# Three attentions of a two-block transformer kernel: order of scores, maximum and normalising, and place of a projection

## The chip, the cores and the metric

One core of one Trainium2 chip runs the whole kernel. The metric is the device time of one execution in microseconds, as a median over runs.

## The reference, cut to what matters

512 tokens of width 1024 pass through two transformer blocks in float32. Three attentions lie in them. The first block has a neighbourhood attention (8 heads of 64; every token sees a window of a grid of 8 rows by 64 columns, with a bias per head) and a dilated one (three window and dilation pairs, merged with weights from their log-sums). The second block opens with a differential attention and a pooling mixer side by side:

```python
proj = h @ ab_w_in[e]
q, k, v, u = jnp.split(proj, [DIFF_WIDTH, 2 * DIFF_WIDTH, 3 * DIFF_WIDTH], axis=-1)
a_out = _diff_attention(q, k, v, ab_lambda[e], ab_subln[e], i)
b_out = _pool_mixer(u, pool_w[e], pool_scale[e])
x = x + jnp.concatenate([a_out, b_out], axis=-1) @ ab_w_out[e]
# _diff_attention, for each block of 128 queries, over the keys up to it
p1 = jax.nn.softmax(jnp.where(mask, s1, -jnp.inf), axis=-1)
p2 = jax.nn.softmax(jnp.where(mask, s2, -jnp.inf), axis=-1)
p = p1 - lam * p2
# _pool_mixer, for each of four groups of 128 channels, w = 2, 4, 8, 16
outs.append((cs - lagged) / count[None, :, None] - ug)
```

`lam` comes from two exponentials of dot products of parameters. The attention's output is normalised per head (rms norm), the pooled groups are each multiplied by a 128 by 128 matrix.

## The kernel before, in words

The program is one instruction stream per engine, ordered by hand, with counting semaphores between them. Activations lie transposed, channels on partitions, 512 tokens along. A matrix product takes weight tiles of 512 KB (128 output columns, 1024 rows) through a ring of four places: SP loads a tile (L413) as soon as PE has counted the tile four earlier as done (`tile_done`); ACT rounds it to the high part (`part`, L1089, called by `parts` at fixed places of its stream); GpSimd subtracts to get the low part (`split`, L554, in order of the tiles); PE then multiplies high by high, high by low and low by high, 24 matmuls of 512 columns for a tile (`three`, L613 to L615, in `linear`).

Each attention has 16 steps and the same frame on three engines (`attention`, one function each). On PE, in turn `i`: scores (i), transposes of the probabilities (i-1) (`turn`), output (i-2). On DVE: normalising (i-1) (`norm_p`), then maximum (i) with the bias or mask added on the way out of PSUM (`smax`, L1501, and the negated maximum, L1512), then the copy out (i-2). On ACT: exponential (i) with its sum (L1163, L1319), then the copy (i-1) of the transposed probabilities out of PSUM (L1168, L1324). Scores lie in two buffers of SBUF and two pairs of PSUM banks (0 to 3), the transposes in banks 4 and 5, outputs in 6 and 7.

In the neighbourhood attention (L723 scores, L732 transposes, L743 outputs) every step has 2 x 256 score columns. Its bias tile is refilled by SP once maximum 4 is done and is used from step 12 on; after maximum 16 SP loads the mask of the dilated one into the same place. The dilated attention (L759, L761, L769, L781) has 768 columns a step. In the differential one (L922, L931, L938) a step is one head of one block of 128 queries; steps 0 to 3 have 128 columns in each of the two halves, steps 4 to 7 have 256, 8 to 11 384, 12 to 15 512. Its normalising is a reciprocal (L1760), one scaling for each half (L1763, L1764, the second with lambda) and their sum (L1767).

Ahead of the differential attention PE makes q, k (8 tiles, T_AB to T_AB+7), v (4 tiles) and then `u`, the input of the pooling (tiles T_AB+12 to T_AB+15, `linear`); ACT copies each out (L1308), takes the lambda exponential (L1311) and rounds tiles T_ABO to T_ABO+3 of the output projection. GpSimd splits all these tiles, waits for `u`, and pools the four groups in a row (L594, L595, L599, L601) while the attention runs. Behind it comes, for each of four heads, square (ACT), mean (PE, L950), root (ACT), reciprocal (DVE, L1780), product (L1784), and the pooled group's matmul (L952) and scaling (L1787); each of the eight chunks is split in a high and a low part (L1444), and the output projection (T_ABO, 8 tiles) starts.

## Time and profile before

| what | value |
|---|---|
| median of 3 runs | 3739.52 us (3739.14 to 3746.37) |
| the profiled execution's own time | 3744.43 us |
| its span, first to last instruction | 3742.6 us |
| busy: PE, DVE, ACT, POOL | 93%, 44%, 32%, 34% |
| mean granted TensorE clock | 0.953 of full |
| chain that ended last: PE, DVE, issue, POOL | 68%, 12%, 11%, 4% |

PE is a stream of matmuls, and its busy share is high nearly everywhere; the share of the other engines says only where they work. "Granted clock" is 1.0 at 2.4 GHz and 0.5 at 1.2 GHz; a value between is a mean over time. A group's "idle before" is the time its engine stood still just ahead of it, with the releaser behind the arrow. GpSimd is called POOL in the rows.

### The profile page before, as it was taken

To read this page: it belongs to the slowest core of one execution; us is meant where nothing else is said; L and a number is where in the kernel's file an instruction comes from. 1 tells how busy PE (TensorE), PEld (TensorE's weight loads), DVE (VectorE), ACT (ScalarE), POOL (GpSimd) and SP (SyncE) were. 2 spreads that over 40 slices of the span, in tenths; PEclk is the share of its full clock that TensorE was granted. 3 is DMA by queue.
4 is the path that set the end of the run, shared out by engine and by line. 5 is a ranking of instruction groups with operands and counts; after the bars stand their busy time and mean duration, and the time that the engine had idled before them with its cause. 6 is when DMAs were issued, how large, how long until landed. Compare 5 with 4: busy or idle time off the path is not lost.

```text
span 3742.6 us, 41725 instructions
## 1 busy us (share of the span) xinstructions
PE 3475.5 (93%) x15884; PEld 2786.2 (74%) x15884; DVE 1633.4 (44%) x2894; ACT 1182.6 (32%) x1640; POOL 1276.2 (34%) x550
## 2 busy tenths in 40 slices
PE   7968999999999999999999998858999997969998
PEld 5665777887888888888888875736888686748886
DVE  5805215996545511455555534073322216153221
ACT  4424223333333333222222223332322333033221
POOL 3320133443333334444444432412444332014442
PEclk9988999999999999999999999978999998589999
DMA  2230132343554565766666631302333221012332
GB/s 104 67 101 23 63 100 71 115 144 107 197 180 173 199 202 167 196 185 188 190 184 187 190 118 57 107 1 68 96 96 96 82 80 34 0 45 90 96 96 79
DMA packets 424646, 428.03 MB, mean 114 GB/s; under 512 B 146720, under 2 KB 343968, under 8 KB 422704
## 3 DMA queue, kind: packets, MB, share of 16 engines
q1 hardware_dynamic: 424496, 425.93, 36.4%
q8 instruction: 106, 1.74, 0.2%
q14 instruction: 44, 0.36, 0.0%
HBM read 354.57 MB, written 69.21 MB: 113 GB/s over the span
## 4 chain that ended last, share of the span: by engine, by line
PE 68%; DVE 12%; issue 11%; POOL 4%; ACT 2%; DMA 1%; SPq 1%; POOLq 0%; DVEq 0%; PEldq 0%; ACTq 0%
PE pb L613 19%; PE pb L615 19%; PE pb L614 19%; POOL s_over L554 4%; PE pb L872 3%; PE pb L630 1%; DVE s_hS L1444 1%; DVE s_sq L1430 1%; PE pb L1048 1%; DMA s_ring<-w 1%; PE pb L796 1%; PE pb L1050 1%; PE pb L1038 1%; DVE s_arena L1651 1%; PE pb L781 1%
## 5 line engine op out<-in xcount | busy, mean ns | idle before, releaser
L554 POOL TENSOR_TENSOR s_over<-s_ring,s_rhigh 128x1024 fp32r<-128x1024 f32 x518 | 1253.4, 2421 | 2430.5 <-ACT s_rhigh L1089 2430.4
L1089 ACT ACTIVATE s_rhigh<-s_ring 128x1024 fp32r<-128x1024 f32 x518 | 548.8, 1060 | 1635.9 <-DMA s_ring<-w 803.8
L613 PE MATMUL pb<-s_hS,s_rhigh 128*128 128x512 f32 x2368 | 953.9, 403 | 81.8 <-DVE s_hS L1444 76.9
L615 PE MATMUL pb<-s_hS,s_over 128*128 128x512 f32 x2376 | 932.1, 392 | 0.0
L614 PE MATMUL pb<-s_hS,s_rhigh 128*128 128x512 f32 x2368 | 929.2, 392 | 0.0
L613 PE MATMUL pb<-s_over,s_rhigh 128*128 128x512 f32 x1600 | 632.4, 395 | 0.0
L615 PE MATMUL pb<-s_over,s_over 128*128 128x512 f32 x1600 | 632.0, 395 | 0.0
L614 PE MATMUL pb<-s_over,s_rhigh 128*128 128x512 f32 x1600 | 631.9, 395 | 0.0
L613 PEld LDWEIGHTS pb<-s_hS,s_rhigh 128*128 128x128 f32 x2368 | 449.5, 190 | 201.3 <-DVE s_hS L1444 65.5
L614 PEld LDWEIGHTS pb<-s_hS,s_rhigh 128*128 128x128 f32 x2368 | 450.4, 190 | 95.3 <-issue 7.0
L615 PEld LDWEIGHTS pb<-s_hS,s_over 128*128 128x128 f32 x2376 | 449.6, 189 | 96.2
L1579 DVE TENSOR_TENSOR s_xT<-pb,s_xT 128x512 f32<-128x512 f32 x216 | 149.5, 692 | 700.9 <-PE pb L615 700.9
L614 PEld LDWEIGHTS pb<-s_over,s_rhigh 128*128 128x128 f32 x1600 | 300.4, 188 | 73.1 <-issue 0.2
L613 PEld LDWEIGHTS pb<-s_over,s_rhigh 128*128 128x128 f32 x1600 | 300.4, 188 | 73.0 <-issue 0.2
L615 PEld LDWEIGHTS pb<-s_over,s_over 128*128 128x128 f32 x1600 | 300.3, 188 | 72.9
L1702 DVE TENSOR_TENSOR s_std<-s_arena 128x512 f32<-128x512 f32 x128 | 254.5, 1988 | 85.0 <-DMA s_arena<-gates 83.4
L1805 DVE TENSOR_TENSOR s_std<-s_arena 128x512 f32<-128x512 f32 x64 | 101.2, 1582 | 232.4 <-ACT s_arena L1277 232.4
L1684 DVE TENSOR_TENSOR s_arena<-s_arena 128x1024 f32<-128x1024 f32 x64 | 87.9, 1373 | 231.5 <-PE pb L872 228.0
L1693 DVE TENSOR_TENSOR s_over<-s_std,s_over 128x512 fp32r<-128x512 f32 x192 | 142.8, 744 | 95.7 <-ACT s_over L1220 94.9
L1687 DVE TENSOR_SCALAR s_arena<-s_arena 128x128 f32<-128x128 f32 x512 | 153.5, 374 | 0.0
L872 PEld LDWEIGHTS pb<-s_arena 128*128 128x128 f32 x1024 | 124.1, 191 | 5.0
L1220 ACT ACTIVATE s_over<-s_std 128x512 fp32r<-128x512 f32 x192 | 118.9, 619 | 26.6 <-DVE s_std L1702 12.4
(234 smaller groups left out, 2863.2 us busy)
## 6 DMA issues: line engine op xcount, KB each, us to landing
s_ring<-w SPq DMA_DIRECT2D x272, 512.0 KB, 3.5
s_ring<-eu SPq DMA_DIRECT2D x128, 512.0 KB, 4.0
s_ring<-ev SPq DMA_DIRECT2D x128, 512.0 KB, 4.1
acts<-s_arena SPq DMA_DIRECT2D x128, 256.0 KB, 4.0
gates<-s_arena SPq DMA_DIRECT2D x8, 4096.0 KB, 13.8
s_arena<-acts SPq DMA_DIRECT2D x128, 256.0 KB, 4.4
s_arena<-gates SPq DMA_DIRECT2D x128, 256.0 KB, 4.5
s_xT<-xT SPq DMA_DIRECT2D x1, 2048.0 KB, 8.2
```

Source lines behind the costliest of these rows:

```text
L554: gp.tensor_tensor(rlow[:, s, :, :], ring[:, s, :, :], rhigh[:, s, :, :].bitcast(F32), ALU.subtract).then_inc(S("w_split"), 1)
L613: mm(dst, a_high, b_high, start=start, stop=False)
L614: mm(dst, a_high, b_low, start=False, stop=False)
L615: return mm(dst, a_low, b_high, start=False, stop=stop)
L872: mm(pb[:, 4 + (t // 4) % 4, (t % 4) * P:(t % 4 + 1) * P], oh2[:, t // 8 % 2, t % 8, :], oh1[:, t % 8, :], start=True, stop=True).then_inc ...
L1089: sc.activation(rhigh[:, s, :, :], ring[:, s, :, :], ACT.Copy).then_inc(S("w_high"), 1)
L1220: sc.activation(actS[:, half, 0, k, :], std[:, k % 2, :], ACT.Copy).then_inc(S("e_high"), 1)
L1579: return ve.tensor_tensor(xT[:, c, :], pb[:, bank, :], xT[:, c, :], ALU.add)\
L1687: ve.tensor_scalar(oh1[:, t % 8, :], iota, chT[:, 0, t:t + 1], chT[:, 2, t:t + 1], ALU.is_equal, ALU.mult).then_inc(S("oh_done"), 1)
L1693: ve.tensor_tensor(actS[:, half, 1, k, :], std[:, k % 2, :], actS[:, half, 0, k, :].bitcast(F32), ALU.subtract).then_inc(S("e_act"), 1)
L1702: ve.tensor_tensor(std[:, e % 2, :], va_in[:, e % 4, :], gtile[:, e % 4, :], ALU.mult)\
L1805: ve.tensor_tensor(std[:, j % 2, :], ga[:, j % 2, :], ga[:, j % 2, :], ALU.mult)\
```

## The change

- PE: scores (0) are issued ahead of the loop; turn `i` issues scores (i+1), transposes (i-1), then a piece of other work where there is one (`beside`), then output (i-2).
- DVE: maximum (i) comes first in a turn, then normalising (i-1), then copy out (i-3). Maximum (i) waits for the transposes that free its buffer: three buffers in the neighbourhood and the differential attention, two in the dilated one.
- The four tiles of `u` are projected in quarters (6 matmuls each) inside the turns of the differential attention, into bank 7; its outputs all use bank 6 and each waits for the copy out before. ACT copies group j out in turn 4 (j+1), and rounds T_ABO to T_ABO+2 in turns 6, 10 and 14 and T_ABO+3 behind the last. GpSimd pools a group when it is there and splits one T_ABO tile after each.
- Differential normalising: the sum of both scaled halves becomes one scaling, a product of two 128 x 1 values and one fused product-and-add.
- Scratch of the part behind the attention moves from `ptmp` to `dsc`, and DVE's wait for all four pooled groups ahead of it goes.

```diff
@@ GpSimd
-            splits(T_AB, T_ABO + RING)
+            splits(T_AB, T_ABO)
             gp.wait_ge(S("pool_in"), 32)
-            gp.wait_ge(S("d_copied"), 20)
             for gi in range(4):
+                gp.wait_ge(S("d_copied"), 16 + gi + 1)
...
                 gp.wait_ge(S("pooled"), gi + 1)
+                splits(T_ABO + gi, T_ABO + gi + 1)
@@ PE
-            def attention(n, s0, scores, turn, outp):
+            def attention(n, s0, scores, turn, outp, beside=None):
+                scores(0).then_inc(S("at_scores"), 1)
                 for i in range(n + 2):
-                    if i < n:
-                        if i >= 2:
-                            pe.wait_ge(S("at_max"), s0 + i - 1)
-                        scores(i).then_inc(S("at_scores"), 1)
+                    if i + 1 < n:
+                        if i >= 1:
+                            pe.wait_ge(S("at_max"), s0 + i)
+                        scores(i + 1).then_inc(S("at_scores"), 1)
                     if 1 <= i <= n:
                         pe.wait_ge(S("at_prob"), s0 + i)
                         turn(i - 1).then_inc(S("at_turned"), 1)
+                    if beside is not None and i < n:
+                        beside(i)
...
-            for i in range(4):
-                pe.wait_ge(S("d_copied"), 4 + i + 1)
-                linear(T_AB + 12 + i, i)
-            pe.wait_ge(S("d_copied"), 20)
+            pe.wait_ge(S("d_copied"), 16)
+            def pool_in(i):
+                j, r = divmod(i, 4)
+                n = T_AB + 12 + j
+                if r == 0:
+                    slot(n)
+                    if j >= 1:
+                        pe.wait_ge(S("d_copied"), 16 + j)
+                for c in range(2 * r, 2 * r + 2):
+                    m = three(pb[:, 7, :], rhigh[:, n % RING, c, :], rlow[:, n % RING, c, :], hS[:, 0, c, :],
+                              hS[:, 1, c, :], c == 0, c == DC - 1)
+                if r == 3:
+                    m.then_inc(S("tile_done"), 1)
...
             def diff_out(s):
+                if s >= 1:
+                    pe.wait_ge(S("at_out"), DIFF0 + s)
                 for b in range(i + 1):
-                    m = mm(pb[:, 6 + s % 2, 0:P], ...
+                    m = mm(pb[:, 6, 0:P], ...
@@ ACT
-            for i in range(4):
-                parts(T_AB + 12 + i + 3)
-                sc.wait_ge(S("tile_done"), T_AB + 12 + i + 1)
-                sc.activation(du[:, i, :], pb[:, i, :], ACT.Copy).then_inc(S("d_copied"), 1)
+            parts(T_AB + 15)
             sc.wait_ge(S("lam_dot"), 1)
             sc.activation(lam[:, 2:4], lam[:, 0:2], ACT.Exp).then_inc(S("lam_exp"), 1)
-            parts(T_ABO + 3)
+            def pool_in(i):
+                if i >= 6 and i % 4 == 2:
+                    parts(T_ABO + i // 4 - 1)
+                if i >= 4 and i % 4 == 0:
+                    j = i // 4 - 1
+                    sc.wait_ge(S("tile_done"), T_AB + 12 + j + 1)
+                    sc.activation(du[:, j, :], pb[:, 7, :], ACT.Copy).then_inc(S("d_copied"), 1)
...
+            parts(T_ABO + 3)
             sc.wait_ge(S("at_out"), DIFF0 + 16)
@@ DVE
-            def attention(n, s0, smax, norm_p, outp):
-                for i in range(n + 2):
+            def attention(n, s0, buffers, smax, norm_p, outp):
+                for i in range(n + 3):
+                    if i < n:
+                        ve.wait_ge(S("at_scores"), s0 + i + 1)
+                        if i >= buffers:
+                            ve.wait_ge(S("at_turned"), s0 + i - buffers + 1)
+                        smax(i)
                     if 1 <= i <= n:
                         ve.wait_ge(S("at_exp"), s0 + i)
                         norm_p(i - 1).then_inc(S("at_prob"), 1)
-                    if i < n:
-                        ve.wait_ge(S("at_scores"), s0 + i + 1)
-                        if i >= 2:
-                            ve.wait_ge(S("at_turned"), s0 + i - 1)
-                        smax(i)
-                    if i >= 2:
-                        ve.wait_ge(S("at_pv"), s0 + i - 1)
-                        outp(i - 2).then_inc(S("at_out"), 1)
+                    if i >= 3:
+                        ve.wait_ge(S("at_pv"), s0 + i - 2)
+                        outp(i - 3).then_inc(S("at_out"), 1)
...
-                ve.tensor_scalar(v1, v1, st2[:, s % 2, 6:7], None, ALU.mult)
-                ve.tensor_scalar(v2, v2, st2[:, s % 2, 7:8], lam[:, 5:6], ALU.mult, ALU.mult)\
-                    .then_inc(S("diff_both"), 1)
+                ve.tensor_scalar(st2[:, s % 2, 5:6], st2[:, s % 2, 7:8], lam[:, 5:6], None, ALU.mult)
+                ve.tensor_scalar(v1, v1, st2[:, s % 2, 6:7], None, ALU.mult).then_inc(S("diff_both"), 1)
                 ve.wait_ge(S("diff_both"), s + 1)
-                return ve.tensor_tensor(v1, v1, v2, ALU.add)
+                return ve.scalar_tensor_tensor(v1, v2, st2[:, s % 2, 5:6], v1, ALU.mult, ALU.add)
...
-            ve.wait_ge(S("pooled"), 4)
-            split(H_CAT, cat, ptmp, cat_chunk, hS)
+            split(H_CAT, cat, dsc[:, 0, :, :], cat_chunk, hS)
```

## Rows read from the trace of the kernel before

**Rows 1.** Stretches: length, PE, PEld, DVE, ACT, POOL busy (instructions), granted clock, DMA
```profile
2399.70:2424.15 24.45, 22.60 (x104) 18.28 (x103) 0.32 (x3) 9.19 (x11) 11.89 (x5) 1.00 0.38 128
2424.15:2499.88 75.73, 39.55 (x176) 24.54 (x176) 53.12 (x160) 25.37 (x81) 24.95 (x29) 0.69 0.00 1
...
269.50:325.04 55.54, 33.38 (x256) 20.43 (x256) 30.95 (x144) 27.64 (x82) 2.34 (x1) 0.89 0.17 58
325.10:401.90 76.80, 73.48 (x384) 58.16 (x384) 39.42 (x144) 29.01 (x49) 0.00 (x0) 0.90 0.00 1
...
333.00:340.00 7.00, 7.00 (x25) 5.24 (x24) 2.14 (x8) 3.29 (x6) 0.00 (x0) 0.50 0.01 2
```

**Rows 2.** DVE's timeline, neighbourhood attention: start, length, engine, line (idle before)
```profile
298.42 0.17 DVE L1526 RECIPROCAL s_arena<-s_arena 128x2 f32<-128x2 f32 x1 [0.40 <-ACT s_arena L1163]
...
299.96 0.17 DVE L1512 TENSOR_SCALAR s_arena<-s_arena 128x2 f32<-128x2 f32 x1
```

**Rows 3.** ACT's timeline, neighbourhood attention, exponential and copy
```profile
300.16 0.51 ACT L1163 ACTIVATE s_arena<-s_arena 128x256 f32<-128x256 f32 x1 [1.29 <-DVE s_arena L1512]
...
301.16 0.57 ACT L1168 ACTIVATE s_arena<-pb 128x512 f32<-128x512 f32 x1
```

**Rows 4.** PE's timeline, neighbourhood attention, transposes and scores
```profile
299.29 0.66 PE L732 MATMUL pb<-s_mats,s_arena 128*128 128x128 f32 x4 [0.98 <-DVE s_arena L1530]
...
300.47 0.70 PE L723 MATMUL pb<-s_arena 64*128 64x256 f32 x4
```

**Rows 5.** PE's timeline, dilated attention, transposes after a wait
```profile
331.53 1.54 PE L769 MATMUL pb<-s_mats,s_arena 128*128 128x128 f32 x6 [1.54 <-DVE s_arena L1556]
...
398.15 0.87 PE L769 MATMUL pb<-s_mats,s_arena 128*128 128x128 f32 x6 [1.33 <-DVE s_arena L1556]
```

**Rows 6.** Timeline of ACT and POOL around the four projections
```profile
2404.11 4.75 POOL L554 TENSOR_TENSOR s_over<-s_ring,s_rhigh 128x1024 fp32r<-128x1024 f32 x2 [7.28 <-ACT s_rhigh L1089]
2404.21 1.06 ACT L1089 ACTIVATE s_rhigh<-s_ring 128x1024 fp32r<-128x1024 f32 x1 [0.17 <-DMA s_ring<-w]
...
2422.23 1.28 ACT L1311 ACT_TABLE_LOAD   x1
```

**Rows 7.** DVE's timeline, differential attention, widest step
```profile
2481.33 0.68 DVE L1501 CUSTOM_DVE_ANT_0 s_arena<-pb,s_arena 128x512 f32<-128x512 f32 x1
...
2482.66 0.17 DVE L1512 TENSOR_SCALAR s_arena<-s_arena 128x2 f32<-128x2 f32 x1
...
2484.62 0.49 DVE L1763 TENSOR_SCALAR s_arena<-s_arena 128x512 f32<-128x512 f32 x1
...
2485.59 0.69 DVE L1767 TENSOR_TENSOR s_arena<-s_arena 128x512 f32<-128x512 f32 x1
```

**Rows 8.** PE's timeline, differential attention, widest step
```profile
2482.72 1.13 PE L922 MATMUL pb<-s_arena 64*128 64x512 f32 x4
...
2491.22 0.66 PE L931 MATMUL pb<-s_mats,s_arena 128*128 128x128 f32 x4 [0.71 <-DVE s_arena L1767]
2491.72 1.06 PE L938 MATMUL pb<-s_arena 128*128 128x128 f32 x8
```

**Rows 9.** DVE beside POOL in the differential attention; groups by line (busy, mean ns)
```profile
2426.14 2.34 POOL L554 TENSOR_TENSOR s_over<-s_ring,s_rhigh 128x1024 fp32r<-128x1024 f32 x1 [2.85 <-ACT s_rhigh L1089]
...
2427.07 1.50 DVE L1763 TENSOR_SCALAR s_arena<-s_arena 128x128 f32<-128x128 f32 x1
...
L1767 DVE TENSOR_TENSOR s_arena<-s_arena 128x128 f32<-128x128 f32 (+3 forms) x16 | 11.4, 716 | 0.5
...
L1763 DVE TENSOR_SCALAR s_arena<-s_arena 128x128 f32<-128x128 f32 (+3 forms) x16 | 8.5, 530 | 0.6
```

**Rows 10.** POOL's additions of the pooling, by line
```profile
L595 POOL TENSOR_TENSOR s_arena<-s_arena 128x511 f32<-128x511 f32 (+3 forms) x10 | 11.1, 1110 | 0.0
```

**Rows 11.** DMA issues of the page: times, KB each, us to landing
```profile
s_ring<-w SPq DMA_DIRECT2D x272, 512.0 KB, 3.5
```

**Rows 12.** DVE's timeline behind the differential attention
```profile
2506.88 0.75 DVE L1784 SCALAR_TENSOR_TENSOR s_arena<-s_arena,s_small,s_rstd 128x512 f32<-128x512 f32 x1
```

More of the change, by code:

```diff
@@ L364, in program @@
         diffm = F.take(T)
-        dsc = F.take(2, 2, T)
+        dsc = F.take(3, 2, T)
         dpt = F.take(2, T)
@@ L1146, in _, with attention @@
             parts(T_GATE + 3)
-            def attention(n, s0, exp, pt):
+            def attention(n, s0, exp, pt, beside=None):
                 for i in range(n + 1):
@@ L1158, in attention @@
                         pt(i - 1).then_inc(S("at_pt"), 1)
+                    if beside is not None:
+                        beside(i)
             def na_exp(s):
                 for e in range(2):
-                    v = sc1[:, s % 2, e * 256:(e + 1) * 256]
+                    v = sc1n[:, s % 3, e * 256:(e + 1) * 256]
                     m = sc.activation(v, v, ACT.Exp, bias=st1[:, s % 2, 2 + e:3 + e],
```

31 lines of the change are left out of this document (16 added, 15 removed).

## The prediction

> **What bounds the kernel now.** I read the stretches first [rows 1]: two of them are not TensorE work at full speed. In the neighbourhood attention (269.5 to 325.0 us) PE is busy 33.4 of 55.5 us, in the differential attention (2424.2 to 2499.9) 39.6 of 75.7 at a mean granted clock of 0.69. The projections ahead of the latter fill PE, and so does the dilated attention (325.1 to 401.9): 73.5 of 76.8.
>
> Why the first waits, by the timelines. DVE's step runs from a reciprocal over two scalings and the next step's maximum to the negation, 1.54 us [rows 2]. ACT starts the exponentials 0.20 us after the negation began, needs 1.0 us for them, then copies for 0.57 us, and had been idle 1.29 us before [rows 3]: a period of 2.87 us. PE idled 0.98 us of it [rows 4]. Nobody is full: it is a ring, normalise (s) -> maximum (s+1) -> exponential (s+1) -> normalise (s+1), because DVE takes the new maximum only after it has normalised the old step. The same ring makes 4.9 us in the widest differential steps.
>
> **The change, part by part.** My sum is made against the profiled execution, 3744.4 us (span 3742.6, 1.8 around it); the median shown is 3739.5, 4.9 lower, and I carry the difference over to it.
>
> *Neighbourhood.* With the maximum first, exponential (i) runs beside DVE's normalising (i-1). Left is the fullest engine. DVE: 1.54 [rows 2], and about 0.1 for the negation (its successor starts before its 0.17 end) and 0.2 for the copy out, both estimates: 1.84 us. PE: transposes and outputs 1.18 together, scores 0.6 to 0.7 [rows 4]: 1.8. ACT 1.57 [rows 3]; its copy waits for the transposes, which end 1.65 us after a negation begins (about 1.0 of DVE, 0.66 of PE), and ends at 2.3; that delays the next exponential by 0.25 us, which has slack. I take 1.9; if ACT's 2.3 decided, 2.3. The first exponential stays where it is, at 276.6, behind a weight rounding. Transposes 0 to 15 then go from 278.5 in 15 x 1.9, plus 2.9 for a low clock at the start (a mean of 0.89 over 55.5 us [rows 1] is 12 us at the half level; I put 7 us of it on the first 2.2 steps, PE-bound there at 3.2): 309.9 against 322.2. **-12.3** (bounds -7 at 2.3 us, -13.5). The third buffer costs nothing (same words). The refill of the bias is issued at maximum 4 and due at 12, 15 us later; twice the size of a weight tile, which lands in 3.5 us [rows 11], it stays hidden.
>
> *Dilated.* PE-bound; two buffers stay. Gone are PE's waits for the first and the last normalisation, 1.54 and 1.33 us [rows 5]: **-2.9** (bounds 0, and -6 with an earlier rise of the clock). The new order adds a wait, maximum (i) behind transposes (i-2); PE has 3.5 us of outputs and scores to do meanwhile, and DVE's chain (maximum, joint maximum, negation, normalising) is about 2.4.
>
> *Differential, start.* The four projections, 22.1 us of PE (22.6 with the first scores [rows 1]), go from ahead to beside. PE is ready at 2399.7. But ACT first rounds tile T_AB+15 until 2405.3, loads a table for 1.28 us and takes the lambda exponential: 2406.8. DVE's lambda sum then meets GpSimd's splits, which run until 2408.9 [rows 6]. So the first maximum comes at 2409.3 instead of 2424.2, and transposes (0) at 2411.9.
>
> *Differential, steps.* PE at full clock, widest step: transposes 0.50, outputs 0.91 without the drain, scores 0.97 [rows 8]; the narrower ones shrink with their 1 to 3 blocks, to 0.13, 0.21 and 0.36: 25.0 us for all 16, with the projections 47.1. From transposes (0) to (15), without what lies outside, 42.3: 2.8 a step, 3.8 for the widest. DVE, widest [rows 7]: maximum 1.33, negation 0.1, reciprocal and small product 0.3, one scaling 0.54, product-and-add 0.65, copy out 0.2: 3.1; narrowest 1.75; 38.8 for all. (The fused form saves one pass, 0.40 in the widest, and adds the small product.) ACT needs 2.0 in the widest. So PE bounds it: 42.3.
>
> *Added to that.* (a) GpSimd: a scaling of 128 elements took 1.50 us and ended as the split that had begun before it did [rows 9]. DVE waits for the running GpSimd instruction. Excess: 16 x (0.530 - 0.385) = 2.3 us for L1763 (clean mean: midway between 0.28, the fastest, and 0.49, the widest [rows 7]), as much each for L1764 and the negation, 16 x (0.716 - 0.495) = 3.5 for L1767 [rows 9]: 10.4 us in 25.0 of GpSimd work [rows 1]. Afterwards three of four poolings (14.9 of 22.6 us) and three splits (7.1) lie within steps 4 to 15: 22 us, so 9.2 of DVE. About half meets steps where PE has 0.4 to 0.7 us to spare: +5. (b) Clock: PE idles from about 2403 to 2409.5, and a full PE ran at 0.5 for 7 us elsewhere (333 to 340 [rows 1]) before the clock rose: +3 (bounds +1, and +18 if it stays low long). (c) hand-offs +1.5. Transposes (15) at 2411.9 + 42.3 + 9.5 = 2463.7; with transposes, copy, output and copy out, 2.8, the attention ends at 2466.5 instead of 2499.9: **-33.4**. The one output bank adds a wait of output (i-2) for copy out (i-3), which DVE does 0.3 us after normalising, while PE has 1.4 us of projection to do: nothing.
>
> The Trainium skill (SBUF — State Buffer, "Who interferes with whom") says of this port that it is an exclusive lock, held for the whole instruction. By that rule alone each of the four DVE instructions would wait for the rest of a GpSimd instruction, and (a) would be about 10 instead of 5: 3699.
>
> *Behind the attention.* ACT has one more rounding (T_ABO+3) ahead of its first square. The tile's load is issued when the last projection is done, 0.9 us before transposes (15), lands 3.5 us later [rows 11] and is rounded in 1.06 [rows 6]: ACT is ready 3.7 us after transposes (15) begin, the last copy out at 2.8: **+1.0**. Pooling 3 (4 x 1.11 [rows 10], four short copies, two of about 1.27: 7.7 us) starts at +1.9 and a split follows it to +12.5. PE needs it 18 us behind the attention: hidden. But L1784, 7.0 us behind the end before [rows 12], falls under that split: **+1.8**. The dropped wait for pooling and the new scratch place free nothing, since pooling had ended 47 us before. SP's order is unchanged; each T_ABO tile is issued when a projection frees its place and is rounded three steps later, and its split has until 18 us behind the attention.
>
> Sum: -12.3 - 2.9 - 33.4 + 2.8 = -45.8. 3744.4 becomes 3698.6; on the median's scale **3694**.
>
> **The rivals.**
> 1. *DVE and GpSimd in lockstep.* The poolings are spread over twelve steps instead of seven. For: the waiting in [rows 9]. If each of 48 instructions waits 0.55 us (half of 1.11), that is 26 us, less 8 of slack: 18 instead of 5, 3707. Against: the mean excess in the trace is 0.3. Chance 0.2.
> 2. *Low clock in the differential attention* until step 8: some 21 us of PE work double, +18 instead of 3, 3709. For: a mean of 0.69 over 75.7 us is 47 us at 1.2 GHz. Against: PE was then idle half the time; now it would be full, and a full PE came back after 7 us. The Trainium skill (TensorE: Matmul & The Clock Gate, "What's actually happening") has sustained work release the clock, which speaks against this rival. Chance 0.12.
> 3. *The neighbourhood's ring only moves to ACT* (normalise -> transpose -> copy -> exponential), 2.3 us: 3700. Chance 0.12.
> 4. *Slower: denser but gappy PE work holds 1.2 GHz in all three attentions.* Steps become PE-bound, 3.24 us in the neighbourhood (48.6 against 43.7: +5), 139 instead of 76.8 for the dilated (+62), 2411.9 + 84.6 + 3.8 = 2500.3 for the differential (+0.4), and 2.8 behind: 3810. It decides from 92 us of additional low clock on, since each costs half. No full PE is low for longer than 7 us in [rows 1]. Chance 0.02.
> 5. *It doesn't do what it says:* a wait that I passed over keeps the old ring in all three. Then only the start of the third is won, 14.9 less 2.8: 3727. Against: each wait above has slack by rows. Chance 0.04.
>
> **The numbers.** Forecast 0.5: 3694. The range reaches rivals 1 to 3 and the better bounds (clock back at once, contention hidden, -8): 3684 to 3711. A measurement of this kernel can tell about 0.2% (7.5 us) from no change. Faster: all but rival 4 and a part of 5: 0.95; same 0.03; slower 0.02.
>
> **What would show it.** Right: transposes of the neighbourhood 1.9 us apart and DVE without idle there; a dilated stretch of 74 us; the third attention's first maximum 15 us (and the win before it) earlier; PE busy over 80% there at a clock near 0.9; DVE instructions of over 1 us at steps 4 to 14; ACT's last rounding just ahead of its first square. Wrong: a period of 2.3 us or more in the first (a ring is left), PE idle with DVE full in the third (rival 1), a clock of 0.5 past its fourth step (rival 2), or more than 31 us from the third attention's end to the output projection.

## The result, and the profile after

The kernel after takes 3683.94 us (median of 4 runs, 3683.55 to 3685.20), the kernel before 3740.47 (4 runs, 3739.14 to 3746.37): a ratio of 0.9846, 95% interval 0.9829 to 0.9864. That is 56.5 us less; forecast were 3694, and 3684 to 3711 as the range. The direction and the waits that go were right; the gain came out 10 us larger than forecast, 0.06 us below the lower end of the range. The profiled execution of after took 3684.18 us (span 3682.4), 60.2 less than that of before.

The same stretches as in [rows 1], from the answer by windows of the kernel after. The first two are the neighbourhood and the dilated attention; then the differential attention from its first scores to its first transposes, from there to its end, and what follows it up to the output projection:

```profile
271.20:310.60 39.40, 31.14 (x256) 19.27 (x256) 28.98 (x144) 27.65 (x82) 2.34 (x1) 0.91 0.23 81
310.60:381.20 70.60, 68.58 (x385) 55.77 (x385) 38.34 (x145) 30.70 (x49) 0.00 (x0) 1.00 0.00 1
2373.90:2386.00 12.10, 3.10 (x18) 2.08 (x19) 4.35 (x17) 5.25 (x12) 4.64 (x2) 0.73 0.23 87
2386.00:2442.20 56.20, 50.06 (x262) 35.68 (x262) 44.65 (x146) 29.83 (x80) 25.23 (x25) 0.97 0.11 38
2442.20:2470.30 28.10, 16.90 (x35) 7.87 (x35) 24.99 (x19) 11.25 (x17) 8.65 (x8) 0.82 0.00 1
```

The dilated attention ran at a granted clock of 1.00 where before had 0.90, the differential at 0.97 where before had a mean of 0.69.

One step of the neighbourhood, DVE's timeline, against [rows 2]:

```profile
290.39 0.42 DVE L1525 CUSTOM_DVE_ANT_0 s_arena<-pb,s_arena 128x256 f32<-128x256 f32 x1
...
291.20 0.17 DVE L1536 TENSOR_SCALAR s_arena<-s_arena 128x2 f32<-128x2 f32 x1
291.28 0.16 DVE L1550 RECIPROCAL s_arena<-s_arena 128x2 f32<-128x2 f32 x1
291.47 0.62 DVE L1554 TENSOR_SCALAR s_arena<-s_arena 128x256 f32<-128x256 f32 x2
292.01 0.28 DVE L1563 COPY s_arena<-pb 128x128 f32<-128x128 f32 x1
292.26 0.42 DVE L1525 CUSTOM_DVE_ANT_0 s_arena<-pb,s_arena 128x256 f32<-128x256 f32 x1
```

None has idle time before it, and PE has none either (busy 19.80 of the 19.80 us from 280.2 to 300.0): the ring is gone, and DVE and PE are level, with a period of 292.26 - 290.39 = 1.87 us (1.82 and 1.87 alternate, a mean of 1.84; forecast 1.9, before 2.87). PE's transposes [rows 4] now follow at once, and ACT's copy [rows 3] waits 0.24 to 0.30 us:

```profile
290.33 0.66 PE L737 MATMUL pb<-s_mats,s_arena 128*128 128x128 f32 x4
```

```profile
291.03 0.60 ACT L1187 ACTIVATE s_arena<-pb 128x512 f32<-128x512 f32 x1 [0.30 <-PE pb L737]
```

In the differential attention the start came out as forecast. ACT's timeline around 2379 us (compare [rows 6]):

```profile
2378.51 1.06 ACT L1106 ACTIVATE s_rhigh<-s_ring 128x1024 fp32r<-128x1024 f32 x1 [0.18 <-DMA s_ring<-w]
2379.59 1.28 ACT L1327 ACT_TABLE_LOAD   x1
```

and DVE's behind it:

```profile
2381.11 1.95 DVE L1770 TENSOR_TENSOR s_arena<-s_arena 128x1 f32<-128x1 f32 x1 [70.03 <-ACT s_arena L1327]
2383.10 0.15 DVE L1772 TENSOR_SCALAR s_arena<-s_arena 128x1 f32<-128x1 f32 x1
2383.29 0.29 DVE L1525 CUSTOM_DVE_ANT_0 s_arena<-pb,s_arena 128x128 f32<-128x128 f32 x1
```

The first maximum comes 9.4 us after PE was ready (2373.9), forecast 9.6. The answer by waits of PE, from 2374 to 2475 us:

```profile
PE pb L937 <- DVE s_arena L1525: 7.6, 1, 7.6
PE pb L946 <- DVE s_arena L1790: 3.5, 6, 1.3
PE pb L615 <- ACT s_arena L1336: 3.2, 3, 1.2
```

The second line is what is left of the 37.0 us that PE waited for normalised scores before (16 waits on the line that [rows 8] shows with 0.71); 1.35 of its 3.5 us lie ahead of transposes (0). The third I had not seen: PE stands about 1 us ahead of each of the projections 1, 2 and 3, until ACT has copied the last one out of the bank that all four share.

**Where the time went.** Each stretch in the profiled executions, from the first or last start of the named instruction. "Ready" is the moment at which PE could begin the differential part (before: its first pooling projection, 2399.5; after: its first scores, 2373.9).

| stretch | before | after | difference | forecast |
|---|---|---|---|---|
| start to first neighbourhood scores | 269.5 | 271.2 | +1.7 | none |
| to first dilated scores | 55.6 | 39.5 | -16.1 | -12.3 |
| to last dilated outputs | 76.1 | 69.7 | -6.4 | -2.9 |
| to ready | 1998.3 | 1993.5 | -4.8 | none |
| ready to last copy out | 100.1 | 68.0 | -32.1 | -33.4 |
| to last pooling product | 19.0 | 19.4 | +0.4 | +2.8 |
| to the end | 1224.0 | 1221.1 | -2.9 | none |

The changed stages gave -54.2 where -45.8 was forecast; stages whose code is the same gave another -6.0. The questions were: what makes the dilated attention twice as much better as forecast, and is the differential's sum right for its own reasons?

### The profile page after: what moved, and what is told of

Its sections match the earlier page's. It is cut to its first block, busy times and chain, and to the rows that moved or that the text cites. A ratio compares the mean times of both kernels' runs of the same rounds, so it can differ in the third digit from the quotient of the medians.

```text
span 3682.4 us, 41719 instructions
## 1 busy us (share of the span) xinstructions
PE 3457.7 (94%) x15884; PEld 2777.1 (75%) x15884; DVE 1631.3 (44%) x2894; ACT 1184.7 (32%) x1640; POOL 1278.1 (35%) x550
## 3 DMA queue, kind: packets, MB, share of 16 engines
q8 instruction: 106, 1.74, 0.2%
## 4 chain that ended last, share of the span: by engine, by line
PE 69%; DVE 12%; issue 11%; POOL 4%; ACT 1%; DMA 1%; SPq 1%; POOLq 0%; DVEq 0%; PEldq 0%; ACTq 0%
PE pb L615 19%; PE pb L617 19%; PE pb L616 19%; POOL s_over L555 4%; PE pb L877 3%; PE pb L632 1%; DMA s_ring<-w 1%; DVE s_hS L1468 1%; DVE s_sq L1454 1%; PE pb L1065 1%; PE pb L801 1%; PE pb L1067 1%; PE pb L1055 1%; DVE s_arena L1669 1%; DVE s_arena L1675 1%
## 5 line engine op out<-in xcount | busy, mean ns | idle before, releaser
L617 PEld LDWEIGHTS pb<-s_over,s_over 128*128 128x128 f32 x1600 | 300.4, 188 | 72.8
L1726 DVE TENSOR_TENSOR s_std<-s_arena 128x512 f32<-128x512 f32 x128 | 262.6, 2052 | 84.9 <-DMA s_arena<-gates 84.4
L1827 DVE TENSOR_TENSOR s_std<-s_arena 128x512 f32<-128x512 f32 x64 | 101.5, 1586 | 232.0 <-ACT s_arena L1296 232.0
```

The source lines that it names most:

```text
L617: return mm(dst, a_low, b_high, start=False, stop=stop)
L1726: ve.tensor_tensor(std[:, e % 2, :], va_in[:, e % 4, :], gtile[:, e % 4, :], ALU.mult)\
L1827: ve.tensor_tensor(std[:, j % 2, :], ga[:, j % 2, :], ga[:, j % 2, :], ALU.mult)\
```

## The experiments

All stretches below are taken as in the table above. A rate of products and a clock are from the same traces.

**1 and 2. The new order in one attention alone.** Both are the kernel before, with the new `attention` beside the old and called in one place, on PE (shown) and on DVE; the first has the neighbourhood's third buffer too:

```
-            attention(16, 0, na_scores, na_turn, na_out)
+            attention1(16, 0, na_scores, na_turn, na_out)
```
```
-            attention(16, DIL0, dil_scores, dil_turn, dil_out)
+            attention1(16, DIL0, dil_scores, dil_turn, dil_out)
```

> The kernel before, with the new order and the third buffer in the neighbourhood attention alone; the dilated and the differential attention as before. Theory (the clock): the neighbourhood stretch, 269.5 to 325.0 us before, shrinks by 15 to 16 us as in the whole change, and the dilated stretch behind it, whose instructions are untouched, shrinks too, from 76.8 to about 74, because PE comes into it from denser work and its clock does not fall: about 3722 us in all. Rival (each order is worth more than I priced): the dilated stretch stays at 76.8 and its granted clock at 0.90, the whole is about 3725.

> The kernel before, with the new order in the dilated attention alone. Theory (the clock): the two removed waits of PE, 1.54 and 1.33 us, are won, 2.9 us, and the low clock at the start stays, so the stretch goes from 76.8 to about 74, and the whole to about 3737.5. Rival: the new order alone, with PE full from the first scores on, brings all 6.3 us: the stretch 70.5, the whole 3734.

Measured, with before at 3744.85 (13 runs): the first 3726.62 (ratio 0.9953, 0.9936 to 0.9969), the second 3738.32 (0.998, 0.997 to 0.9989). The stretches say more than the totals. With the new order in the neighbourhood alone, that took 39.3 us (55.6 before), the whole gain there, and the dilated attention 75.1 (-1.0). With the new order in the dilated alone, that took 74.1 (-2.0). Together they had given -6.4: more than both. (The second kernel's profile is of its slowest execution, 3748.19, so its total is no guide here.) The clock shows why. PE by windows, the first kernel, then the second:

```profile
309.90:318.00 8.10, 5.75 (x20) 0.73 0.00 0
318.00:326.00 8.00, 8.00 (x30) 0.63 0.01 3
```

```profile
325.30:333.00 7.70, 7.68 (x21) 0.50 0.00 0
333.00:341.00 8.00, 8.00 (x30) 0.53 0.01 3
```

The new order in the dilated alone does fill PE from its first microsecond (7.68 of 7.70), and yet runs its first 15 us at 1.2 GHz: the clock was down before the stage began. It had not been down in the neighbourhood's steps, each with a wait of 1 us; the windows of the kernel before have 1.00 there. In the kernel before it fell at 323.0 us, 0.8 us behind the neighbourhood's last wait, which is longer (1.62 us), and rose at 340.1; in this one it did both 0.4 us later, with the same last wait (1.61 us). PE by windows, the kernel before:

```profile
302.00:322.90 20.90, 13.23 (x114) 1.00 0.09 27
323.10:340.00 16.90, 14.95 (x58) 0.50 0.06 26
```

The new order in the neighbourhood alone comes in at the full clock and loses it in the old first wait, which PE's timeline shows (the clock was 0.50 from 313.7 to 323.9 us):

```profile
315.46 1.54 PE L790 MATMUL pb<-s_mats,s_arena 128*128 128x128 f32 x6 [2.35 <-DVE s_arena L1592]
```

With both, PE's longest wait from 303 us to the end of the dilated attention is 0.9 us, and the clock stays at 1.00. The gain in the dilated stage is a joint one. Both expectations held in direction. In the first kernel the dilated attention lies between theory and rival (75.1 us; about 74 and 76.8), since the clock did fall there; in the second it is the theory's.

**3 and 4. Order and projections in the differential attention, apart.** Kernel 3 is after with the old step order there, the projections still beside; kernel 4 is after with the projections ahead, as before, and the new order. Only PE's part is shown; DVE's order goes with it in kernel 3, ACT's copies and GpSimd's poolings and splits in kernel 4:

```
-            attention(16, DIFF0, diff_scores, diff_turn, diff_out, pool_in)
+            attention0(16, DIFF0, diff_scores, diff_turn, diff_out, pool_in)
```
```
-            attention(16, DIFF0, diff_scores, diff_turn, diff_out, pool_in)
+            for i in range(4):
+                pe.wait_ge(S("d_copied"), 4 + i + 1)
+                linear(T_AB + 12 + i, i)
+            attention(16, DIFF0, diff_scores, diff_turn, diff_out)
```

> The changed kernel with the old order of scores, maximum and normalising in the differential attention; the projections stay beside it. Theory: the ring of normalise, maximum, exponential comes back at 3.4 to 4.9 us a step, 16 steps from the earlier start, with the projections hidden in it: attention from 2373.9 to about 2455 instead of 2442, the whole about 3697. Rival (PE's work is the bound either way, since the projections fill the ring's gaps): within 3 us of the changed kernel, 3684 to 3687.

> The changed kernel with the four projections ahead of the differential attention again (with all of GpSimd's poolings in a row, as before); the new order stays. Theory: the attention starts some 15 us later, and its steps then cost 1.8 to 3.1 us of DVE (38.8 in all) plus GpSimd's delays at the first steps, 45 to 50 us instead of 58: the whole about 3690 to 3692, so that the placing beside is worth 6 to 8 us behind the order. Rival (the placing is most of the gain): 3698 or more.

Measured: 3711.00 (0.991, 0.9893 to 0.9926) and 3698.72 (0.9876, 0.986 to 0.9893). From ready to the last copy out: before 100.1, old order with projections beside 94.0, new order with projections ahead 80.0 (22.8 of projections and 57.2), both 68.0. So the order is worth 26.0 with the projections beside, and the projections beside 12.0 with the new order. The two other steps, from the kernel before, are not clean: both kernels also have the fused form of the normalising (experiment 10), so 20.1 is order and fused form, 6.1 projections and fused form.

Both kernels were slower than my theories. The fourth reached the 3698 of its rival, though the placing is not most of the gain; its steps took 57.2 us where 45 to 50 were expected. The third was worse than either figure. Its DVE waits tell:

```profile
DVE s_arena L1828 <- PE pb L974: 34.2, 15, 6.8
```

In the old order DVE copies an output out before it takes the next maximum, and PE's outputs now stand behind a quarter of a projection: each projection quarter lies inside the ring. The projections beside need the new order.

The fourth has the other lesson. PE by windows in its differential attention:

```profile
2400.00:2420.00 20.00, 10.37 (x36) 0.50 0.00 0
2420.00:2430.00 10.00, 8.58 (x35) 0.60 0.01 2
```

With the projections ahead PE is half idle in the narrow steps, and the clock stays at 0.50 for 20 us and more. This is the low clock of my rival 2, and it does exist: with the projections beside it ends 3.8 us behind the first transposes.

**5 and 9. The clock by itself.** The kernel before, its orders untouched, with products that nobody reads in PE's waits (`fill(bank, count)` multiplies the identity by constants `count` times). The first try:

```
+                        if s0 == 0 and i >= 4:
+                            pe.wait_ge(S("at_max"), s0 + i)
+                            fill((i + 1) % 2 * 2, 6 if i < 16 else 12)
+                        if s0 == DIL0 and i == 1:
+                            fill(5, 18)
                         pe.wait_ge(S("at_prob"), s0 + i)
```

> The kernel before, its orders untouched; TensorE is given matrix products into unused space, whose results nobody reads, in its waits of the last twelve neighbourhood steps (0.7 us each, 1.4 us in the last) and in its first wait of the dilated attention (2.1 us). In the kernel before the clock is 0.50 and 0.56 from 325 to 341 us, with 14.4 us of TensorE work in it, so 7 of it are lost. Theory (the low clock is the term I mis-sized, and the new order mends it by filling TensorE): the clock stays up, the dilated stretch shrinks from 76.8 to between 70.5 and 73 us although its order is the old one; the neighbourhood stretch stays at 55 to 57. Whole kernel 4 to 6 us faster than before. Rival (the new order itself saves the waits and the clock only follows): the dilated stretch stays at 75 us or more, and the kernel within 2 us of before.

Measured: 3765.19, slower than before (1.0054, 1.0037 to 1.007). The filling was four times too long. I had priced it by the weights' products, which are of the rounded type; the constants are full float32, and the line answer of the filler has two records for each of the 102 products:

```profile
L702 PE MATMUL pb<-s_mats x204: 379/379/796, 288.9 to 361.8; 128*128 128x256 f32 x102
```

Six of them filled 2.7 us, 0.45 us each for 256 columns. The run has one more thing to show. PE by windows in its dilated attention:

```profile
349.30:352.40 3.10, 3.07 (x12) 1.00 0.00 0
352.50:355.50 3.00, 3.00 (x8) 0.50 0.00 0
```

The clock fell in the middle of full work, 3 us behind a wait of 0.40 us. So waits are not the whole of it; what made it fall here stays open.

The filling was then cut to size (128 columns; 3, 6 and 9 of them):

> As clock_fill, with the products that nobody reads cut to size: of 128 columns (0.22 us each by the 0.45 us that one of 256 columns took there), three in each of the neighbourhood's steps 4 to 15, six in the last, nine in the first wait of the dilated attention. Theory (the low clock is the mis-sized term): the neighbourhood stretch stays near 55.6 us, the clock stays up from there into the dilated attention, and that shrinks from 76.8 to 70.5 to 73 us with its old order; the kernel is 4 to 6 us faster than before. Rival (the order itself): 75 us or more, and the kernel within 2 us of before.

Measured: 3734.92 (10 runs), before 3739.16 (15 runs), ratio 0.9988, 0.9975 to 1.0001. The total alone would not settle it; the stretch does. PE from the first dilated scores to the end of that attention:

```profile
328.60:401.40 72.80, 70.64 (x402) 1.00 0.00 1
```

Neighbourhood 55.2 us (the fill cost nothing there), clock 1.00 from 300 us on, and 72.8 for the dilated attention with its old order and old waits, against the 76.80 of [rows 1]. The clock alone is worth 4.0 of the 6.4 us; the other 2.4 are left for the waits that the new order removes. The fill went into the waits of twelve steps, the neighbourhood's last and the dilated's first at once, so it doesn't tell which of them lets the clock fall; the trace of before points at the last one (above).

**6. GpSimd out of the way.** The kernel after without the pooling arithmetic on GpSimd:

```
-                for lvl in range(gi + 1):
-                    ...
-                gp.tensor_tensor(du[:, gi, :], src, du[:, gi, :], ALU.subtract).then_inc(S("pooled"), 1)
+                gp.tensor_copy(ptmp[:, 0, 0:1], du[:, gi, 0:1]).then_inc(S("pooled"), 1)
```

> The kernel after, without the pooling on GpSimd (its additions, its product with the counts and its subtraction are left out; the projected values go on unpooled); its four weight splits stay. Theory (term (a), 5 us forecast for DVE instructions that wait for GpSimd, two thirds of it poolings): the differential attention's transposes (0) to its end shrink from 55.9 to about 52.5 us, and behind the attention DVE's split of a chunk no longer waits 1.4 us: 3679 to 3681 in all. Rival (TensorE bounds these steps, and VectorE's waits lie under its work): less than 1.5 us in the attention, 3682 to 3684 in all.

Measured: 3687.02 (0.9846, 0.983 to 0.9863), no faster than after; transposes (0) to the end of the differential attention 57.0 us, after 55.9. DVE, however, had really been held up; its busy time in that stretch is 38.96 us here:

```profile
2386.90:2444.00 57.10, 38.96 (x146) 0.95 0.11 38
```

against 44.65 in the kernel after (the fourth of the windows above): 5.7 us of waiting for the poolings. My term (a) had DVE's side right in size (9.2 us for poolings and splits, two thirds of it poolings: 6.2).

The equal total looks as if this waiting had been free. The steps say otherwise. Transposes (13) begin 44.1 us behind transposes (0) here and 46.2 in the kernel after: 2.2 us won, and up to there PE waits for no normalised scores any more. Then one of GpSimd's weight splits, which this kernel keeps, begins with DVE's product-and-add. PE, DVE and POOL, by timeline:

```profile
2436.29 0.66 PE L935 MATMUL pb<-s_mats,s_arena 128*128 128x128 f32 x4 [2.39 <-DVE s_arena L1779]
```

```profile
2433.33 2.90 DVE L1779 SCALAR_TENSOR_TENSOR s_arena<-s_arena 128x512 f32<-128x512 f32 x1
```

```profile
2433.34 2.35 POOL L555 TENSOR_TENSOR s_over<-s_ring,s_rhigh 128x1024 fp32r<-128x1024 f32 x1 [9.27 <-ACT s_rhigh L1095]
```

It took 2.90 us for 0.75, PE stood 2.39 us, and the clock was at 0.50 from 2438 to 2440 us. In the kernel after the same split holds up a scaling one step later (1.59 us for 0.48), and PE waits 0.38 us. So the total decides neither for the theory nor for the rival: the poolings cost the kernel after 2.2 us up to transposes (13), of 3.4 expected in all, and one collision took them back here.

What such a wait looks like in the kernel after, POOL's timeline and then DVE's:

```profile
2412.81 1.30 POOL L602 TENSOR_TENSOR s_arena<-s_arena 128x512 f32<-128x512 f32 x1
```

```profile
2412.86 1.28 DVE L1536 TENSOR_SCALAR s_arena<-s_arena 128x2 f32<-128x2 f32 x1
2414.05 0.15 DVE L1784 RECIPROCAL s_arena<-s_arena 128x2 f32<-128x2 f32 x1
```

A negation of two elements, 0.17 us elsewhere, took 1.28, and ended as GpSimd's product did.

**7. The low clock at the starts.** The kernel after, with fills in PE's two long waits, ahead of the first transposes of the neighbourhood and around the third scores of the differential attention:

```
+                        if s0 == DIFF0 and i == 1:
+                            fill(5, 30, 0)
...
+                        if s0 == 0 and i == 1:
+                            fill(7, 50)
+                        if s0 == DIFF0 and i == 1:
+                            fill(5, 5, 0)
```

> The kernel after; TensorE is given matrix products that nobody reads in its two long waits, 5.9 us of the 6.7 ahead of the first transposes of the neighbourhood, and 7.0 of the 7.6 us ahead of the third scores of the differential attention with 1.2 us ahead of its first transposes. Theory (what is left of the clock terms can be had by keeping TensorE busy): the clock is 1.0 from the first transposes on, the differential attention ends 2.5 to 3.5 us earlier (work of 5.6 us ran at the half level there), the neighbourhood 1 to 1.5 us: 3679 to 3681 where the kernel after has 3683.9. Rival (DVE or ACT bounds the first steps, so a faster TensorE only waits): under 1 us each, 3682 to 3684.

Measured: 3718.66 (0.9936, 0.992 to 0.9953). It carries the same fault of size as the first fill (the fill ahead of the neighbourhood's first transposes alone took 21.9 us), so its total says nothing on the two theories. Behind the fills the clock is 1.00, and there the stretches can be read:

```profile
294.10:323.10 29.00, 27.77 (x246) 1.00 0.22 74
2417.00:2471.20 54.20, 48.38 (x263) 1.00 0.12 40
```

From the first transposes on the neighbourhood took 29.0 us where after took 30.5, the differential 54.2 where after took 55.9. Of my allowances for the clock, 2.9 and 3, after really lost 1.5 and 1.7. The second row also gives PE's work at the full clock, 48.4 us, where I had counted 45.1 (42.3 and 2.8).

**8. ACT's copy of a projection ahead of its copy of the transposes**, so that PE's three waits of about 1 us go:

```
                         exp(i).then_inc(S("at_exp"), 1)
+                    if ahead is not None:
+                        ahead(i)
                     if i >= 1:
                         sc.wait_ge(S("at_turned"), s0 + i)
```

> The kernel after; ScalarE copies a finished pooling projection ahead of its copy of the transposes, not behind it, in the turns 4, 8 and 12, where it is idle for the transposes anyway. Theory (TensorE's waits of about 1 us ahead of projections 1, 2 and 3 are a cost of the change, 3.2 us in the trace): they go, and TensorE bounds the steps, so 2 to 3 us: 3681 to 3682. Rival (these waits only take the place of TensorE's next wait for DVE's normalising, which is late because of GpSimd): under 1 us, 3683 to 3684.

Measured: 3685.36 (0.9839, 0.9822 to 0.9855), the stretch 56.3 us where after had 55.9. The waits for ACT are gone from the answer, and the wait for normalised scores has grown from 3.5 to 6.0 us:

```profile
PE pb L946 <- DVE s_arena L1795: 6.0, 7, 1.7
```

The rival holds in the main: the wait only changed its name. A part is the clock: in this profile poolings held up two DVE instructions of one step (1.25 and 1.44 us), PE stood 1.74 us behind them, the clock fell after it, and PE's busy time is 51.2 us where after had 50.1.

**10. The fused form undone** (the differential's normalising with two scalings and an addition again):

```
-                ve.tensor_scalar(st2[:, s % 2, 5:6], st2[:, s % 2, 7:8], lam[:, 5:6], None, ALU.mult)
-                ve.tensor_scalar(v1, v1, st2[:, s % 2, 6:7], None, ALU.mult).then_inc(S("diff_both"), 1)
+                ve.tensor_scalar(v1, v1, st2[:, s % 2, 6:7], None, ALU.mult)
+                ve.tensor_scalar(v2, v2, st2[:, s % 2, 7:8], lam[:, 5:6], ALU.mult, ALU.mult)\
+                    .then_inc(S("diff_both"), 1)
                 ve.wait_ge(S("diff_both"), s + 1)
-                return ve.scalar_tensor_tensor(v1, v2, st2[:, s % 2, 5:6], v1, ALU.mult, ALU.add)
+                return ve.tensor_tensor(v1, v1, v2, ALU.add)
```

> The kernel after, with the old normalising of the differential attention: two scalings and an addition in place of a small product, one scaling and the fused product-and-addition. It adds 0.40 us to DVE's widest step and takes the small product of 0.2 from every one. Theory (TensorE bounds these steps, as no_pooling and copy_ahead showed): the stretch from transposes (0) to the end of the differential attention stays within 1 us of 55.9, and the kernel at 3684 to 3686. Rival (DVE's chain from maximum to normalised scores bounds the steps): 3 us or more in the stretch, 3687 or above.

Measured: 3693.81 (4 runs, 3693.48 to 3695.67; 0.9884, 0.9869 to 0.9899), and the stretch from transposes (0) to the end 61.6 us, 5.7 more than after. My theory fell. DVE is busy 50.71 us of it, and PE's wait for it is 7.8:

```profile
2386.40:2448.00 61.60, 50.71 (x145) 0.95 0.11 35
```

```profile
PE pb L946 <- DVE s_arena L1791: 7.8, 7, 2.5
```

So PE and DVE are nearly level in these steps: PE 50.1 and DVE 44.7 of 56 us in the kernel after, and 6 us more for DVE is paid nearly in full: 4.2 us as PE's waits for DVE, 1.4 as PE's work at a lower clock (busy 51.5 us for 50.1). PE's longest wait, 2.48 us, is again behind an instruction held by a split (2.72 us for 0.69). In the steps whose transposes begin at 2401.6, 2404.6 and 2407.7, where none was held, PE did not wait at all. The fused form, which I had entered as a saving of 0.40 in a step that something else bounds, is what keeps DVE on the cheap side: in place of a scaling that GpSimd held up here to 1.28 and 1.35 us it has a product of two 128 x 1 values, 0.21 us each time.

**11, 12 and 13. Three moves on ScalarE.** The two long waits at the starts are ACT's queue: a rounding and a table load stand ahead of the first exponential. The edit, cut:

```
+                if i == 1:
+                    sc.wait_ge(S("lam_dot"), 1)
+                    sc.activation(lam[:, 2:4], lam[:, 0:2], ACT.Exp).then_inc(S("lam_exp"), 1)
...
-            parts(T_AB + 15)
-            sc.wait_ge(S("lam_dot"), 1)
-            sc.activation(lam[:, 2:4], lam[:, 0:2], ACT.Exp).then_inc(S("lam_exp"), 1)
...
+            sc.activation(spare[:, 0:1], eps, ACT.Exp)
...
-            parts(T_GATE + 3)
...
+            sc.activation(spare[:, 1:2], eps, ACT.Sqrt)
```

> The kernel after, with three moves on ScalarE. (1) The lambda exponential goes ahead of the projections of the differential attention, so that its table load of 1.28 us, the rounding ahead of it and VectorE's sum behind it no longer stand before the first maximum; the rounding of the last projection's tile goes behind the third exponential. (2) The table of the exponential is loaded ahead of the neighbourhood attention by an exponential of one column, and the rounding that stood ahead of it goes behind the fourth. (3) The table of the square root is loaded ahead of the last rounding in the same way. Theory (in both attentions the first transposes wait for ScalarE's queue, not for the scores): first transposes of the neighbourhood 4 to 5.5 us earlier, of the differential attention 7 to 9 us earlier with a clock that hardly falls (1 to 2 us more), the tail 1.3 us shorter: 3668 to 3673. Rival (TensorE and the loads behind the moved roundings are late instead, and take it back): 3678 to 3684.

Measured: 3681.23 (5 runs; 0.9851, 0.9837 to 0.9864). The first scores to the first transposes took 3.8 us instead of 9.0 in the neighbourhood and 3.3 instead of 12.1 in the differential, as expected; but the stretches behind them grew by 2.0 and 1.6 us, where the moved roundings, and the splits that follow them on GpSimd, met DVE. The total lies in the rival's range. The moved roundings were then placed elsewhere:

```
-                      lambda i: parts(T_GATE + 3) if i == 3 else None)
+            attention(16, DIL0, dil_exp, dil_pt, lambda i: parts(T_GATE + 3) if i == 2 else None)
...
-                if i == 2:
-                    parts(T_AB + 15)
+                if i in (1, 3):
+                    parts(T_AB + 14 + i // 2)
```

> As act_early, with the moved roundings placed where its trace left room. There the rounding behind the fourth exponential of the neighbourhood was followed by a GpSimd split over VectorE's scalings (TensorE waited 1.7 us, and the granted clock fell for a step), and the two roundings behind the third exponential of the differential attention held up the fourth by 2 us. Now the first stands behind the third exponential of the dilated attention, and the two others behind the second and the fourth of the differential. Theory (these collisions gave the gain back): first transposes of the neighbourhood to the first dilated scores in 30.5 us as in the kernel after, where act_early took 32.5; differential transposes (0) to the end in 55 to 56, where act_early took 57.5; 3676 to 3679. Rival (moving the work only moves the collision): 3680 or above.

> The kernel after, unchanged, on the same chip and in the same rounds as act_early2, so that the two can be told apart within a few tenths of a per cent. If the three moves on ScalarE are worth what the stretches say, it lies 5 to 8 us above act_early2; if act_early's gain was swallowed by how unchanged stages happen to fall, it lies within 3 us of it.

Measured in the same rounds: 3680.78 (5 runs, 3679.05 to 3690.99; 0.984, 0.9825 to 0.9855) against 3688.64 for the kernel after (4 runs, 3685.50 to 3698.84; 0.9864, 0.9848 to 0.9881). The medians are 7.9 us apart, just over what can be told, and the intervals still touch. The two profiled executions agree on where it comes from: first neighbourhood scores to first dilated scores 33.0 against 39.2, ready to the last copy out 58.6 against 69.0, together -16.6. The clock stays at 1.00 from 2370 us on. The span is only 4.7 shorter: it took 3.4 more ahead of the neighbourhood, 7.5 more between the dilated attention and ready, and the tail 1.0 more. The first two hold a moved instruction each (a table load, the lambda exponential), but the spread is as large: kernels whose code is untouched there took from 269.4 to 273.4 us for the one and from 1991.0 to 2003.8 for the other. So the stretches held as expected, and the total, at the edge of the rival's 3680, does not tell the version clearly from the kernel after. The square root's table, loaded early, gained nothing: it moved ACT's last rounding behind it, and the first square waited 0.6 us for that.

## Why the prediction was right or wrong

The waits and the periods were right. What failed is how the low clock was charged: 2.9 us in the neighbourhood, where it cost 0.9 to 1.5, and as a loss that stays in the dilated attention, where 4.0 us came back. The changed stages gave 8.4 us more than forecast: 3.8 in the first, 3.5 in the second and 2.4 behind the attention more, 1.3 in the third less; the rest of the 10 us is the spread of unchanged stages.

- **Neighbourhood, -12.3, measured -16.1.** The mechanism and the period held (1.9 forecast, 1.84 measured, 0.9 us over 15). From transposes (0) to (15) 31.4 us were forecast and 28.1 came. Most of the gap is "plus 2.9 for a low clock at the start": slowed by it were only the first two steps, at 2.20 and 2.38 us, 0.9 over the mean, and then the clock was up; the last step, with no maximum left to take, was 0.5 shorter. The row that I took for evidence, a mean clock of 0.89 over the old stretch, was that of a kernel whose PE waited in every step.
- **Dilated, -2.9, measured -6.4. This is the step that failed.** The waits were about right (2.0 in experiment 2, a remainder of 2.4 in experiment 9). I kept the low clock of [rows 1] (0.50 from 333 to 340) as a fact of that stage and put its loss into a bound, "-6 with an earlier rise of the clock". It was a consequence of work ahead of it: the clock fell behind the neighbourhood's last wait (experiment 2), or, with that gone, in the dilated's own first wait (experiment 1). Both went with the change. Filling PE's waits in the kernel before, with nothing else changed, gave 4.0 us. Why the clock falls at one wait and not at another is not shown.
- **Differential, -33.4, measured -32.1**, by terms of which two were wrong in opposite directions. First maximum: right within 0.2 us. From transposes (0) to the end 54.6 were forecast and 55.9 came. The 55.9 are PE's work at the full clock, 48.4 us, at least 3.3 more than I had counted; the clock, 1.7 for the forecast +3 (experiment 7); and PE's waits: 3.2 for the shared bank, 2.2 for DVE and 0.5 for the output bank. GpSimd's +5 sits in those 2.2, and experiment 6 leaves its worth open: 2.2 us for the poolings up to transposes (13), the splits not tested. Experiment 8 shows that the waits for the bank and for DVE largely replace each other. That the one output bank costs nothing held (0.5 us of waiting in all); that the one bank of the projections would make PE wait I had not seen, and it cost nothing beyond the other wait.
- **Behind the attention, +2.8, measured +0.4.** ACT's last rounding ended before the last copy out (+0 for +1.0). The instruction under the split was not the one named but the one behind it, DVE's split of a chunk, 2.06 us for 0.69:

```profile
2449.70 2.06 DVE L1468 TENSOR_TENSOR s_hS<-s_arena,s_hS 128x512 fp32r<-128x512 f32 x1
```

  That is +1.4 for +1.8, and the higher clock gave 0.9 back ahead of it.
- **Rival 1** (lockstep) is out: it wanted 26 us of waiting on DVE and 3707, and experiment 6 has 5.7 us for the poolings. The Trainium skill's rule that I had weighed there (SBUF — State Buffer, "Who interferes with whom": an exclusive lock for the whole instruction) is borne out by the trace in the single instruction, 1.28 us for 0.17, and in which instructions wait; it gives DVE's time, not the kernel's: of DVE's 5.7 us PE felt 2.2 up to transposes (13).
- **Rival 2** (low clock in the differential) did not come: the row of 2389.5 to 2442.2 us is at 1.00. It would have, with the projections left ahead (experiment 4). My argument against it, that a full PE gets its clock back, held here (3.8 us behind the first transposes) and is a reason that the two parts of the change belong together. As a rule it was luck: I had leaned on "no full PE is low for longer than 7 us", and experiment 2 has 15 us of full PE at 0.50 to 0.53.
- **Rivals 3, 4 and 5** are out by the period of 1.84 us, the clock of 1.00 and the waits that went.
- **The range** took the better bounds of the third attention alone (-8). With those of the first two, -1.2 and -3.1, also in my text, its lower end would have been about 3682. It also left out what unchanged stages do. The kernel after, profiled twice, took 269.6 and 271.2 us ahead of the neighbourhood and 1225.5 and 1221.1 behind the tail. A total that is a sum over changed stages has several us on top that no row of the change explains; by how little the measured time missed the range is chance.

## What to carry to other kernels

A step order that lets the next step's maximum go first turned a ring of engines into a pipeline here, and then the fullest engine decides; price it by each engine's own instructions in one step, as was done here for the neighbourhood within 4%. But a low granted clock in a stage is not a property of the stage: find in the trace where it fell and what stood ahead of that point, and whether the change removes it, since then the next stage gets cheaper too. When two engines are nearly level, don't read "Y is free" off an unchanged total: removing 5.7 us from DVE won 2.2 and lost them again in one collision with a split; adding 6.1 cost 5.7. Read such runs step by step.

## What the runs showed of the hardware

- TensorE at full load does not have to run at the full clock soon: 15 us of back-to-back work at 1.2 GHz in experiment 2, 8.4 us in experiment 1 (315.5 to 323.9), 3.5 and 3.8 us in the kernel after (from 280.2 and from 2386.0).
- The clock stayed at 1.00 through waits of 1 us in every step (before, 302 to 322.9 us), fell behind one of 1.62 us (323.0) and inside one of 2.35 us (experiment 1), and fell once with TensorE full for 3 us (first fill, 352.4). What decides is not shown.
- A product of float32 constants took 0.45 us for 256 columns, 1.76 ns a column; the weights' products of the rounded type follow each other every 0.23 us for 512 columns, 0.45 ns a column, at the same clock: a factor of 3.9. The Trainium skill (FP8 and Floating Point Precision, "TensorE Precision Notes") gives four passes for true FP32; the trace agrees.
- A DVE instruction of two elements waited for a whole GpSimd instruction (1.28 us), and a product-and-add waited 2.90 us for 0.75. The reciprocal of two elements and the maxima that read PSUM did not: 157 and 516 ns with the poolings, 156 and 517 without.
- Unchanged code took from 269.4 to 273.4 us ahead of the neighbourhood in the profiles of kernels that are the same up to there, and from 1991.0 to 2003.8 between the dilated attention and ready.
